# Where a state-space scan's input matrices are made: turned per batch on TensorE, or spread by loads from a scratch

## The reference, cut to what matters

```python
dt = exp(log_dt); mag = exp(lr * dt)
ar = mag * cos(li * dt); ai = mag * sin(li * dt)        # one decay a per group and state
bbr = kr[..., None] * br - ki[..., None] * bi           # B, scaled
bbi = kr[..., None] * bi + ki[..., None] * br
xr = einsum('blgh,gph->blgp', uf, bbr)                  # u enters the states
xi = einsum('blgh,gph->blgp', uf, bbi)
h[l] = a * h[l-1] + x[l]                                # complex scan over 256 tokens
y = einsum('blgp,ghp->blgh', hr, c_re) - einsum('blgp,ghp->blgh', hi, c_im)
y = gelu(y + d * u);  y = y * sigmoid(y @ w_glu + b_glu)
```

## Time and profile before

| what | us |
|---|---|
| median of 3 runs | 955.41 |
| lowest, highest of the 3 | 952.98, 956.44 |
| the profiled execution | 956.4 |
| its span, first to last instruction | 954.7 |
| PE busy in the span | 936.0 (98%) |
| DVE, ACT, POOL busy | 619.7, 569.7, 112.3 |

### The profile page before, as it was taken

One profiled execution on the slowest core, in us unless ns is written; L12 is line 12 of the kernel. 1 busy time (PEld: TensorE's weight loads), 2 busy tenths in 40 slices (PEclk: granted clock), 3 DMA queues, 4 the chain that ended last, 5 costly groups with the idle time before them and its releaser, 6 DMA issues.

```text
span 954.7 us, 15737 instructions
## 1 busy us (share of the span) xinstructions
PE 936.0 (98%) x5939; PEld 796.4 (83%) x5939; DVE 619.7 (65%) x961; ACT 569.7 (60%) x920; POOL 112.3 (12%) x126
## 2 busy tenths in 40 slices
PE   7999999999999999999999999999999999999998
PEld 7988888778878999888888788888888888888886
DVE  4678989899898964755644555555455555555453
ACT  4689786875957745645545564555455644564332
POOL 3100102002030000000002640220021002200000
PEclk9999999999999999999999999999999999999999
DMA  8776534435344367555999996668999866655662
GB/s 280 185 189 198 156 117 149 134 118 185 110 126 149 113 205 274 182 176 187 178 167 180 185 249 166 188 177 155 168 164 169 202 175 176 177 171 158 210 214 85
DMA packets 116007, 165.83 MB, mean 174 GB/s; under 512 B 19301, under 2 KB 56298, under 8 KB 115690
## 3 DMA queue, kind: packets, MB, share of 16 engines
q1 hardware_dynamic: 99504, 159.67, 64.0%
q10 hardware_dynamic: 16442, 5.33, 2.3%
HBM read 162.86 MB, written 2.11 MB: 173 GB/s over the span
## 4 chain that ended last, share of the span: by engine, by line
PE 80%; DVE 8%; ACT 5%; DMA 3%; issue 2%; POOL 1%; ACTq 0%; SPq 0%; DVEq 0%
PE bank L455 21%; PE bank L457 21%; PE bank L456 21%; PE bank L482 3%; PE bank L483 3%; PE bank L484 3%; DVE wl L976 2%; PE bank L599 1%; ACT wh L968 1%; ACT res L1077 1%; DVE scr L1736 1%; PE bank L591 1%; DMA raw<-in_e_w_in 1%; DMA res<-in_x 1%; PE bank L665 1%
## 5 line engine op out<-in xcount | busy, mean ns | idle before, releaser
L976 DVE TENSOR_TENSOR wl<-raw,wh 128x1024 fp32r<-128x1024 f32 x295 | 361.7, 1230 | 247.5 <-ACT wh L968 246.2
L968 ACT ACTIVATE wh<-raw 128x1024 fp32r<-128x1024 f32 x295 | 310.6, 1058 | 195.0 <-PE bank L457 126.6
L455 PE MATMUL bank<-wh,xh 128*128 128x512 f32 x768 | 307.1, 400 | 1.4 <-DVE wl L976 1.4
L457 PE MATMUL bank<-wh,xl 128*128 128x512 f32 x768 | 300.0, 391 | 0.0
L456 PE MATMUL bank<-wl,xh 128*128 128x512 f32 x768 | 299.2, 390 | 0.0
L457 PEld LDWEIGHTS bank<-wh,xl 128*128 128x128 f32 x768 | 144.1, 188 | 31.1
L455 PEld LDWEIGHTS bank<-wh,xh 128*128 128x128 f32 x768 | 144.4, 188 | 30.2 <-DVE wl L976 1.8
L456 PEld LDWEIGHTS bank<-wl,xh 128*128 128x128 f32 x768 | 144.5, 188 | 27.6
L455 PE MATMUL bank<-wh,yh 128*128 128x512 f32 x256 | 100.5, 393 | 0.0
L457 PE MATMUL bank<-wh,yl 128*128 128x512 f32 x256 | 99.7, 390 | 0.0
L456 PE MATMUL bank<-wl,yh 128*128 128x512 f32 x256 | 99.6, 389 | 0.0
(11 more groups left out here) (319 smaller groups left out, 1027.4 us busy)
## 6 DMA issues: line engine op xcount, KB each, us to landing
raw<-in_o_w_in SPq DMA_DIRECT2D x128, 512.0 KB
raw<-in_e_w_in SPq DMA_DIRECT2D x130, 256.0 KB, 3.2
raw<-in_e_w_out SPq DMA_DIRECT2D x32, 512.0 KB
raw<-in_o_w_out SPq DMA_DIRECT2D x32, 512.0 KB
raw<-in_e_w_in SPq DMA_DIRECT2D x31, 512.0 KB
raw<-in_s_w_glu SPq DMA_DIRECT2D x8, 512.0 KB
res<-in_x SPq DMA_DIRECT2D x8, 256.0 KB, 6.9
res<-in_x SPq DMA_DIRECT2D x1, 2048.0 KB, 9.7
```

Source lines behind the costliest of these rows:

```text
L455: nc.tensor.matmul(o, l_hi, w_hi, start=first, stop=False)
L457: mm = nc.tensor.matmul(o, l_lo, w_hi, start=False, stop=last)
L968: nc.scalar.activation(wh[:, j % RING, :], raw[:, j % RING, :], ACT.Copy).then_inc(hi_done, 1)
L976: nc.vector.tensor_tensor(wl[:, j % RING, :], raw[:, j % RING, :], wh[:, j % RING, :].bitcast(F32), ALU.subtract).then_inc(lo_done, 1)
```

## The change

In words:

- Powers 1 to 4 of a are turned by PE once (`p_rows_turn`, 2 transposes, iteration 1 of the first step) and B once (`b_rows_turn`, 4 transposes each in iterations 2 and 3). ACT copies them to SBUF (`rows_out_of`, iterations 2 to 4), writes them to scratch tensors in DRAM with 20 DMAs from its queue (`rows_keep`, iteration 5), waits for these, and loads back what batch 0 needs with 12 DMAs that repeat rows over the partitions (`rows_load(0)`, iteration 7).
- `rows_load(i + 1)`, again 12 DMAs from ACT's queue, is at slot -1 of batch i.
- DVE multiplies B's rows and the powers' rows already in their turned form (`s5_rows`, 6 operations of 128x512 a batch, slots -4 and -3), ACT spreads the products to `xin` (`s5_spread`, 4 copies, slots -3 and -2). `s5_powers`, `s5_turn` and `s5_turned` go.
- B's powers in `xin` are now 1 to 4, those of C 0 to 3: the state is kept one token further. `s5_far` makes three powers in place of five; the copy of C itself and of B for `s5_near` is ACT's (`s5_own`, 4 copies, slot -6), `s5_pad` copies 512 columns in place of 640.
- `s5_hold` moves from DVE to ACT (8 copies of 64 columns, slot -3).
- `b_blocks` moves from iteration 3 to iteration 0 of the first step. `s5_low` of all batches moves to the last two chunks of layer 0.

```diff
-TAB_SLOT, FAR_SLOT, BA_SLOT = [0, 0], [-7, -4], [-10, -4]
-T_SLOT = [-2, -1, -1, -1]
-NEAR_SLOT, HOLD_SLOT, SKIP_SLOT = [-1, 2], -3, -8
+TAB_SLOT, FAR_SLOT, BA_SLOT = [0, 0], [-7, -4], [-4, -3]
+ROWS_SLOT, SPREAD_SLOT = -1, [-3, -2]
+NEAR_SLOT, HOLD_SLOT, SKIP_SLOT, OWN_SLOT = [-1, 2], -3, -8, -6
+LOW_SLOT = {10: 0, 11: 1, 13: 2, 15: 3}
...
+        b_rows = nc.dram_tensor("b_rows", (2, 16, 2, GP, 64), F32).ap()
+        p_rows = nc.dram_tensor("p_rows", (HOP, 2, 2, GP, 64), F32).ap()
...
-            def s5_turn(i, k):
...
-                o = (xb, yb)[k % 2]
-                for e in range(2):
-                    for r in range(2):
-                        at = (2 * e + r) * P
-                        mm = nc.tensor.transpose(o[:, at:at + P], ba[:, r, 2 * k + e, :], ident)
-                mm.then_inc(t_ps, 1)
...
+            def p_rows_turn():
+                pe.wait_ge(pw_done, 1)
+                for r in range(2):
+                    mm = nc.tensor.transpose(scb[:, r * P:(r + 1) * P], pw[:, r, 1:HOP + 1, :].rearrange("p k i -> p (k i)"), ident)
+                mm.then_inc(bp_ps, 1)
+            def b_rows_turn(half):
+                pe.wait_ge(bc_b, 1)
+                for b in range(2):
+                    for r in range(2):
+                        at = (2 * r + b) * P
+                        mm = nc.tensor.transpose((xb, yb)[half][:, at:at + P], bc_all[:, 2 * half + b, r, :], ident)
+                mm.then_inc(bp_ps, 1)
...
+                        if first and s == 1:
+                            p_rows_turn()
+                        if first and 2 <= s < 4:
+                            b_rows_turn(s - 2)
                         if first and 3 <= s < UNITS - 1:
                             c_turn(s - 3)
...
+            def rows_keep():
+                act.wait_ge(bp_sb, 3)
+                for k in range(HOP):
+                    act.dma_start(p_rows[k, :, :, :, :].rearrange("g r i n -> i (g r) n"),
+                                  st_p[GP * k:GP * (k + 1), :, :, :].rearrange("p g r n -> p (g r) n")).then_inc(bp_out, 16)
+                for k in range(TB):
+                    for g in range(2):
+                        act.dma_start(b_rows[g, :, :, k:GP:TB, :].rearrange("h f b n -> h (f b) n"),
+                                      st_b[16 * k:16 * (k + 1), :, :, g, :].rearrange("p f b n -> p (f b) n")).then_inc(bp_out, 16)
+            def rows_load(i):
+                act.wait_ge(bp_out, 16 * 20)
+                act.wait_ge(xin_sb, 2 * i)
+                tiles = slice(TB * i, TB * i + TB)
+                for k in range(HOP):
+                    for g in range(2):
+                        at = slice(32 * k + 16 * g, 32 * k + 16 * g + 16)
+                        src = p_rows[k, g, :, tiles, :].rearrange("r i n -> r (i n)")
+                        act.dma_start(p_of[at, :, :], src.rearrange("(o r) n -> o r n", o=1).to_broadcast([16, 2, TB * 64]))\
+                            .then_inc(bt_in, 16)
+                    act.dma_start(b_t[32 * k:32 * k + 32, :, :],
+                                  b_rows[:, :, :, tiles, :].rearrange("g h f i n -> (g h) f (i n)")).then_inc(bt_in, 16)
+            def s5_spread(i, r):
+                act.wait_ge(made_done, 2 * i + (r + 1))
...
+                for g in range(2):
+                    ins = nc.scalar.activation(xin[:, :, r, 64 * g:64 * g + 64], made[r].rearrange("p (i n) -> p i n", i=TB),
+                                               ACT.Copy, scale=of_group[:, g:g + 1])
+                ins.then_inc(xin_sb, 1)
...
+                    if ROWS_SLOT == at and i + 1 < DA_PAIRS:
+                        rows_load(i + 1)
...
+            def s5_rows(i, r):
+                (pr, pi), (br, bi) = ([x[:, k, :] for k in range(2)] for x in (p_of, b_t))
+                if r == 0:
+                    dve.wait_ge(bt_in, 16 * 12 * (i + 1))
+                    first, second = prod[0].rearrange("p r n -> p (r n)"), prod[1].rearrange("p r n -> p (r n)")
+                else:
+                    first, second = pr, pi
+                v.tensor_tensor(first, pr, (br, bi)[r], ALU.mult)
+                link(v.tensor_tensor(second, pi, (bi, br)[r], ALU.mult))
+                v.tensor_tensor(made[r], first, second, ALU.add if r else ALU.subtract).then_inc(made_done, 1)
...
-                     (1, 6): b_factors, (1, 7): powers, (2, 2): lam_end, (2, 3): b_blocks}
+                     (1, 6): b_factors, (1, 7): powers, (2, 0): b_blocks, (2, 2): lam_end}
```

More of the change, by code:

```diff
@@ L725, in s5_out_y @@
                     mm.then_inc(y_ps, 1)
[L727 to L731, removed]
             def beside(n, s, heads):
[L734 to L737, removed]
+                s5(n, s)
                 for a, at in heads:
                     attention(a, at)
-                if turns:
-                    s5(n, s)
             def s5(n, s):
@@ L1079, in s5_near, with s5_own, s5_hold @@
                 ins.then_inc(near_sb, 1)
+            def s5_own(i):
+                if i:
+                    act.wait_ge(y_ps, i)
+                    act.wait_ge(near_ps, 2 * i)
+                else:
+                    act.wait_ge(zeros, 1)
+                    act.wait_ge(bc_b, 1)
+                    act.wait_ge(bc_c, 4)
+                for r in range(2):
+                    nc.scalar.activation(cc[r][:, :, 0, :], bc_all[:, i, 2 + r, :].rearrange("p (i h) -> p i h", h=16), ACT.Copy)
+                for g in range(2):
+                    at = slice(64 * g, 64 * g + 64)
+                    ins = nc.scalar.activation(b0[at, :, :, 16 * g:16 * g + 16],
+                                               bc_all[at, i, 0:2, :].rearrange("p r (i h) -> p r i h", h=16), ACT.Copy)
+                ins.then_inc(b0_done, 1)
+            def s5_hold(i):
+                act.wait_ge(h_done, 2 * i) if i else act.wait_ge(prm_exp, 3)
+                for t in range(TB):
+                    ins = nc.scalar.activation(mg[:, t, :], later, ACT.Copy, scale=mag_all[:, TB * i + t:TB * i + t + 1])
+                ins.then_inc(hold_done, 1)
             def s5_pad(i, r):
+                act.wait_ge(b0_done, i + 1)
                 act.wait_ge(cc_done, 2 * i + (r + 1))
                 if r == 0:
[L1085 removed]
+                    act.wait_ge(y_ps, i) if i else act.wait_ge(zeros, 1)
                 for g in range(2):
                     at = slice(64 * g, 64 * g + 64)
[L1088 removed]
+                    dst = ca[at, r, :, :].rearrange("p i (k h) -> p (i k) h", k=HOP)[:, :, 16 * g:16 * g + 16]
                     ins = nc.scalar.activation(dst, cc[r][at].rearrange("p i k h -> p (i k) h"), ACT.Copy)
@@ L1109, in s5 @@
                         table(i)
-                    for k in range(4):
-                        if T_SLOT[k] + 1 == at:
-                            s5_turned(i, k)
+                    if OWN_SLOT == at:
+                        s5_own(i)
+                    if HOLD_SLOT == at:
+                        s5_hold(i)
+                    for r in range(2):
+                        if SPREAD_SLOT[r] == at:
+                            s5_spread(i, r)
+                    if ROWS_SLOT == at and i + 1 < DA_PAIRS:
+                        rows_load(i + 1)
                     for h in range(2):
@@ L1758, in s5 @@
                         if BA_SLOT[part] == at:
-                            s5_powers(i, part)
+                            s5_rows(i, part)
                     if at == SKIP_SLOT:
                         s5_skip(i)
-                    if at == HOLD_SLOT:
-                        s5_hold(i)
                     for h in range(2):
@@ L1768, in s5 @@
                             rotate_out(i, h)
-                    if HIGH_SLOT + 1 == at:
-                        s5_low(i)
+                if n == DA_PAIRS and s in LOW_SLOT:
+                    s5_low(LOW_SLOT[s])
             def log_steps():
```

128 lines of the change are left out of this document (57 added, 71 removed).

## The result

The changed kernel takes 978.1 us, median of 4 runs (976.4 to 979.1), against 955.9 us for 4 runs of the kernel before beside it: ratio 1.024, 95% interval 1.022 to 1.026, 22 us slower. I had forecast 961, so the sign was right and the size was not: 6 us were forecast and 22 came. The profiled execution took 979.1 us with a span of 977.0, the one before 956.4 with 954.7. The mean granted clock of TensorE fell from 1.000 to 0.984.

The account below looks back on a forecast made before the run. PE, busy 98% of the span, was taken to bound the kernel. First step +12.3, three boundaries 3 x 0.3, batch 3 -2.6 and L563 -4.5 gave +6.1 us on 955.4: about 961, range 946 to 981.

Parts of the forecast that it names:

- first step: Layer 0's first step, claimed to end 12.3 us late from the earlier `b_blocks`, a turn of B and ACT's DMA issues.
- next three (3 x 0.3 and L563): Boundaries of batches 0 to 2: 0.3 us lost at each; the wait at L563, 4.5 us in all, gone.
- batch 3 and all behind it: Batch 3 has no load behind it, so it was to keep its full gain of 2.6 us.
- My walk: Order of events on ACT and PE at slots -1 and 0: L695 can start at 235.9 + 12d, PE ready about 238.0.
- PE's turns: PE at step boundaries: dropped transposes (2.3 us) and a wait of 0.28 ahead of L695 give up to 2.6 a batch.
- the wait at L563: PE's wait for DVE's L1846 at the attention output's turn, three times, 4.5 us in all, claimed to go entirely.
- `b_blocks`: DVE in the first step: moved ahead of unit 3's low part, it was to start that unit 4.1 us late.
- The issue time d: Time of each back-to-back DMA issue on ACT, taken as 0.42 us, with ends of 0.28 and 1.08.
- the queue backs up: Rival: issues on a queue with much outstanding are slow, d = 0.6, +18.4 us, 974; chance 0.17.
- Slot -1 of batch 0: First of three boundaries with ACT's 12 load issues, priced like the others at 0.3 us lost.
- "The clock ... plays no part": Layer 0's steps: clock read as 1.00, the upper level, in all stretches, so no term was given to it.
- The rule weighed: ACT issues meeting SP's wait for a shared lock, adding 5.2 us, a sum of +11 instead of +6; left to a rival.

Follow-up runs that it names:

- e4: The changed kernel with the loads of batches 1 to 3 left out, those batches computing with batch 0's rows: 957.7 us.
- e1: The kernel before, with only DVE's `b_blocks` moved from (2, 3) to (2, 0): 961.4 us.
- e7: The changed kernel with 28, 14 and 14 extra unused matmuls on PE ahead of its waits at L708 in batches 0, 1 and 2: 975.2 us.
- e5: The changed kernel with ACT issuing the 36 loads of batches 1 to 3 three an iteration at slots -9 to -6: 960.7 us.
- e3: The changed kernel with the 36 loads of batches 1 to 3 issued by SP between its weight loads: 960.6 us.
- e10: The changed kernel with all 68 new DMAs on SP, but the first step's issues thinned out and ACT issuing the last 4 writes: 956.6 us.
- e11: e10 with `b_blocks` on DVE at (2, 2) instead of (2, 0) and B's turns behind PE's units 4 and 5: 954.9 us.
- e12: e11 with the chain from B's turns to batch 0's loads a unit and more shorter: 950.6 us.
- e6: The kernel before, with 12 extra tiny DMAs issued by ACT in a row at slot -1 of batches 0, 1 and 2: 972.8 us.

## Why the prediction was wrong

By the distances of the table, my terms against what they came to (us):

```
                                      forecast             measured
first step                            +12.3                +15.5
next three (3 x 0.3 and L563)         +0.9 - 4.5 = -3.6     +9.7
batch 3 and all behind it             -2.6                  -0.6
start of the steps                     0                    -2.2
sum                                   +6.1                 +22.4
```

The large miss, 13.3 us, is in the three distances over the step boundaries. My walk had PE wait 240.9 - 238.0 = 2.9 us at each, 8.7 in all; it waited 15.2, which is 6.5 more, and the clock behind the waits took 6.7. The time lies inside my range of 946 to 981 only because that range left room for dear issues; no term of it held the clock or a batch 0 later than the others.

**PE's turns, and the wait at L563: right.** 2.6 us a batch and 4.5 us in all were forecast; steps of 57.6 against 62.3 in e4 show both.

**`b_blocks`: right in its place and price, short of its tail.** Measured from the same point on DVE, unit 3 starts 4.1 us later, as forecast. The whole cost is 5.7 (e1), with the lower clock behind the wait.

**The issue time d: mis-sized.** I took 0.42 us from a range of 0.28 to 1.08. The writes of B take 0.62, the loads of B 0.55, those of powers 0.60 right behind a load of B and 0.45 behind one of their own: 12.3 us for 20 and 6.5 for 12 where I had 8.4 and 5.0. The rows that I took it from were single issues and SP's; of the rivals, "the queue backs up" had d = 0.6 and 974 us. In the first step another error paid for part of this. I let the loads wait for a landing of 5.7 us; the writes landed in 2.2 and the loads followed as soon as ACT came to them. So unit 10 started at 103.75, 13.5 us late by the same anchor against 11.4 forecast. (At d = 1.08 my own walk comes to 33.5 for the first step, not 32.7; the forecast doesn't hang on it.)

**Slot -1 of batch 0: wrong.** I priced all three boundaries alike, 0.3 us each. In batch 0 ACT had not made up for the first step: its issues began at 122.58, 8.7 us behind the first turn of q and k, against 6.0 in batches 1 and 2, and the wait at L708 is 7.4 us, of which e4 leaves 2.4. In batches 1 and 2 it is 3.9; at d = 0.54 my walk gives 235.9 + 6.5 = 242.4 against 238.0 for PE, 4.4.

**"The clock ... plays no part": the step that failed most.** I read a clock of 1.00 in the stretches of before and carried it over to a kernel to which my own walk gave waits of 2 to 4 us. Behind each wait PE runs on at a lower clock. Three stretches of the changed kernel's first step in which PE is busy throughout (columns as above):

```profile
75.00:80.00 5.00, 5.00 (x22) 3.99 (x21) 2.03 (x2) 2.49 (x6) 0.00 (x0) 0.73 0.96 302
95.00:100.00 5.00, 5.00 (x17) 4.00 (x16) 1.23 (x1) 1.41 (x2) 0.00 (x0) 0.68 0.86 193
105.00:110.00 5.00, 5.00 (x16) 3.92 (x15) 4.00 (x9) 4.94 (x10) 1.70 (x2) 0.66 0.69 198
```

At a clock of 0.73 five us do the work of 3.65, so in the three 1.35 + 1.6 + 1.7 = 4.65 us of work are left undone. Most of that is not lost time, for PE waits for ACT and DVE behind it all the same. From the unit at 103.75 to the second one behind it e7 has 7.29 us like the changed kernel, with a clock of 1.00 in place of 0.66 and waits of 0.65 and 0.56 us. From the unit at 94.60 to the one at 103.75, which starts when ACT's loads are out, e7 has 8.7 us against 9.15, although its clock is 0.50 there. Only the first stretch shows in the time: e5, whose first step is the same program and whose clock was 1.00 in its place, has a first distance 1.7 us shorter than the changed kernel and 1.0 shorter than e3. At the boundaries the distance from L708's first group to its second is 13.4, 14.2 and 14.6 us, and 11.8 without a wait, as before: 6.7 us. So the clock has some 8 of the 22 us. Shown by a run made for it are the 4.6 of the 6.7 that e7 takes back by nothing but keeping PE at work; the rest is read from the traces. With the 6.7 left out the change would be some +16, and the issue time and the late batch 0 are what is left against the forecast's +6.

**The rule weighed.** The Trainium skill, Perfetto Trace Analysis, DMA Instruction — HWDGE, would have made issues longer by a wait for a lock when SP's and ACT's meet. For ACT's issues the changed kernel's trace doesn't agree. Second loads of powers took 0.445 us at 188.64 and 252.62, with issues of SP's beside them for 0.38 us, and 0.445 at 124.64 and 190.34 with none; a write of B took 0.62 in either case. Of the 18 weight issues of SP's that ran beside one of ACT's in the steps, 15 took their usual 0.37 or 0.47 us and three took 0.55 to 0.68. The sum is thus not to be raised by the rule's 5 us.

**What stays open.** 2 to 3 us between e4 and the others lie in the next layer, at a wait for POOL. Why an issue in a row costs 0.45 for one shape and 0.62 for another was not tried.

## What to carry to other kernels

A DMA issue is work of the engine that issues it: count it at about half a microsecond, whatever it moves, and put it where that engine waits anyway; twelve in a row, three times, just ahead of a copy that PE needs cost 18 us here, and nothing when they stood three an iteration where it had room. Price a new wait of over 2 us on a nearly full PE at its length and, as an estimate from the three boundaries here, 1.6 to 2.8 us more for the clock behind it. When a change brings a long chain over a scratch (turn, copy, write, load, product), start it as early as its inputs allow and look at its last link: spreading the issues alone (e10) brought nothing in the runs, starting `b_blocks` late and shortening the chain (e11, e12) did.

## What the runs showed of the hardware

- PE's clock after a wait is not settled by the wait's length alone. Waits of 1.95 and 1.98 us at L563 left it at 1.00 before, and one of 1.99 did so in e1; the next one of 1.99 in e1, in the same place one step later, was followed by 0.66 and 1.6 us lost, and in e6 those of 1.97 and 1.98 were each followed by 0.66. Waits of 1.7 to 1.8 us at the boundary in e10 and e12 left it at 1.00 too, one of 1.85 in the changed kernel's first step did not. Each wait of 2.2 us or more in these steps was followed by a lower clock; but the waits for POOL in the next layer left it at 1.00 with 2.53 us in the changed kernel, 2.34 in e10 and 2.39 in e12, and not with 2.43 in e11 or 2.28 in e7.
- An issue of 0.5 KB (0.47 us) costs nearly as much as one of 128 KB (0.55).
- An ACT issue beside one of SP's took no longer than one alone (0.445 us for the same load in both cases).
- Writes of 32 KB to a scratch in DRAM landed in 2.2 us (median), where the single one of the kernel before took 5.7.
